# Moving the first layer's token sums of squares behind the fifth weight piece on the scalar engine

## The reference

```python
def rms_norm(x, g):
    xf = x.astype(jnp.float32)
    y = xf * lax.rsqrt(jnp.mean(xf * xf, axis=-1, keepdims=True) + RMS_EPS)
    return (y * g.astype(jnp.float32)).astype(x.dtype)

h = rms_norm(x, norm_g)
proj = jnp.einsum('bsd,de->bse', h, w_in)
(q_lat, kv_lat, z_a, dn_qkv, dn_a, dn_b, z_b, dil_qkv, z_c, gate_logits) = split_last(proj, IN_SPLITS)
...
mixed = jnp.sum(gates * branch_out, axis=2)
return x + jnp.einsum('bsd,de->bse', mixed, w_out)
```

## Time and profile before

| | |
|---|---|
| time, median of 3 runs (us) | 794.68 |
| time of the profiled execution (us) | 795.01 |
| its span, first to last instruction (us) | 793.0 |
| TensorE busy | 783.8 us, 99% |
| VectorE busy | 556.5 us, 70% |
| ScalarE busy | 478.9 us, 60% |
| GpSimd busy | 194.2 us, 24% |
| granted TensorE clock, mean | 1.000 |

### The profile page before, as it was taken

The page is one execution under the profiler, slowest core; times in us unless marked ns, Lnnn a source line. Parts: engine busy times, 40 slices in busy tenths (PEclk is TensorE's granted clock), DMA queues, the critical chain, the costliest instruction groups (busy, mean ns, idle before and its releaser), DMA issues.

```text
span 793.0 us, 15698 instructions
## 1 busy us (share of the span) xinstructions
PE 783.8 (99%) x6314; PEld 674.7 (85%) x6314; DVE 556.5 (70%) x748; ACT 478.9 (60%) x1077; POOL 194.2 (24%) x196
## 2 busy tenths in 40 slices
PE   7999999999999999999999999999999999999998
PEld 5999888878888888888899998888888888888886
DVE  6687878968376577676656887887865754957763
ACT  5769486676486554354457777765856756543551
POOL 1165104206032002421023511321331500116100
PEclk9999999999999999999999999999999999999999
DMA  8566454454563446465565563554455443654551
GB/s 236 194 191 210 158 145 136 146 160 129 140 185 114 140 126 197 122 196 173 157 196 179 157 197 111 166 171 147 125 156 149 122 146 107 185 185 141 181 184 54
DMA packets 73054, 125.15 MB, mean 158 GB/s; under 512 B 9757, under 2 KB 17047, under 8 KB 72983
## 3 DMA queue, kind: packets, MB, share of 16 engines
q1 hardware_dynamic: 72560, 124.10, 51.2%
q10 hardware_dynamic: 423, 0.06, 0.1%
HBM read 122.03 MB, written 1.05 MB: 155 GB/s over the span
## 4 chain that ended last, share of the span: by engine, by line
PE 93%; ACT 3%; DMA 1%; DVE 1%; issue 1%; SPq 0%; ACTq 0%
PE bank L781 23%; PE bank L783 22%; PE bank L782 22%; PE bank L763 3%; PE bank L765 3%; PE bank L764 3%; PE bank L872 2%; PE bank L925 1%; PE bank L811 1%; DMA raw<-in_w_in 1%; ACT w_hi L1162 1%; PE bank L886 1%; PE bank L920 1%; PE bank L902 1%; PE bank L1013 1%
## 5 line engine op out<-in xcount | busy, mean ns | idle before, releaser
L1500 DVE TENSOR_TENSOR w_lo<-raw,w_hi 128x1024 fp32r<-128x1024 f32 (+4 forms) x240 | 296.4, 1265 | 102.4 <-ACT w_hi L1162 100.1
L1162 ACT ACTIVATE w_hi<-raw 128x1024 fp32r<-128x1024 f32 (+4 forms) x239 | 234.7, 1018 | 83.7 <-PE bank L783 70.2
L781 PE MATMUL bank<-w_hi,hT 128*128 128x512 f32 (+2 forms) x704 | 278.0, 395 | 1.5 <-DVE w_lo L1500 0.7
L783 PE MATMUL bank<-w_hi,hT 128*128 128x512 f32 (+2 forms) x704 | 270.9, 385 | 0.0
L782 PE MATMUL bank<-w_lo,hT 128*128 128x512 f32 (+2 forms) x704 | 270.6, 384 | 0.0
L781 PEld LDWEIGHTS bank<-w_hi,hT 128*128 128x128 f32 x704 | 132.9, 189 | 26.8 <-issue 1.1
L783 PEld LDWEIGHTS bank<-w_hi,hT 128*128 128x128 f32 x704 | 132.7, 188 | 25.7
L782 PEld LDWEIGHTS bank<-w_lo,hT 128*128 128x128 f32 x704 | 133.0, 189 | 22.9
L1948 POOL TENSOR_TENSOR sm<-sm,tab 128x8 f32<-128x8 f32 (+3 forms) x46 | 58.9, 1280 | 183.4 <-ACT dn L1375 78.9
L763 PE MATMUL bank<-hT,w_hi 128*128 128x256 f32 x192 | 54.9, 286 | 0.0
L765 PE MATMUL bank<-hT,w_lo 128*128 128x256 f32 x192 | 54.3, 283 | 0.0
(11 more groups left out here) (236 smaller groups left out, 1000.3 us busy)
## 6 DMA issues: line engine op xcount, KB each, us to landing
raw<-in_w_in SPq DMA_DIRECT2D x168, 512.0 KB, 4.5
raw<-in_w_branch SPq DMA_DIRECT2D x24, 512.0 KB, 4.3
raw<-in_w_out SPq DMA_DIRECT2D x16, 512.0 KB, 4.2
raw<-in_w_in SPq DMA_DIRECT2D x8, 384.0 KB, 5.3
raw<-in_w_in SPq DMA_DIRECT2D x8, 320.0 KB, 4.6
raw<-in_mla_w_kv_b SPq DMA_DIRECT2D x8, 256.0 KB, 3.1
raw<-in_mla_w_q_b SPq DMA_DIRECT2D x4, 384.0 KB, 3.4
xs<-in_x SPq DMA_DIRECT2D x2, 512.0 KB, 5.6
```

The lines of the kernel that those rows point to most:

```text
L781: mm(o, src[0][:, a, tok], hi[:, k, :], start=starts and p == k == 0, stop=False)
L783: last = mm(o, src[1][:, a, tok], hi[:, k, :], start=False, stop=ends(u, p) and k == k1 - k0 - 1)
L1162: av(view(w_hi, q % SPLIT, k1 - k0, n), view(raw, q % RAW, k1 - k0, n), ACT.Copy).then_inc(hi_done, 1)
L1500: tt(view(w_lo, q % SPLIT, k1 - k0, n), view(raw, q % RAW, k1 - k0, n), view(w_hi, q % SPLIT, k1 - k0, n).bitcast(F32), ALU.subtract).then ...
```

## The change

The step `norm` of the first layer is taken out of the beginning of the list and put behind the `prep` of piece 4. The second layer's `norm` stays where it is.

```diff
     order = [(0, ("prep", 0, 0)), (0, ("xT", 0)), (0, ("prep", 0, 1)), (0, ("xT", 1)), (0, ("prep", 1, 0)), (0, ("prep", 1, 1)),
-             (0, ("xT", 2)), (0, ("xT", 3)), (0, ("norm",))]
+             (0, ("xT", 2)), (0, ("xT", 3))]
...
             order.append((layer, ("unit", u, 1)))
             order += ahead(layer, u, 0)
+            if u == layer == 0:
+                order.append((layer, ("norm",)))
             if whole(u) or UNITS[u][2] == 1:
```

## The result

The changed kernel takes 796.34 us, median of 20 runs (795.59 to 797.82); the kernel before, timed beside it, 794.60 us, median of 20 runs (794.07 to 795.88). The ratio is 1.0022 with a 95% interval of 1.0016 to 1.0028: 1.75 us slower, 1.3 to 2.2 by the interval. The prediction said 796.0, between 794.4 and 797.4, +1.3, and gave 0.63 to "no change that can be told" and 0.35 to "slower". The time lies in the range; the loss was put 0.45 us too small, and with it the ratio fell on the far side of the 0.2% line, to which the prediction had given 0.35 (the interval holds the line itself). Three of the 20 executions lie at 797.7 to 797.8, the rest at 795.6 to 796.7. The profiled execution is one of the three: 797.77 us, with a span of 795.7.

A forecast was written before the change was run, and what follows sets the result against it. TensorE was taken as the bound. The sixth piece's first matmul 1.22 us later plus 0.07 of pitch gave +1.3 us, so 796.3 for the profiled execution and 796.0 on the median of 794.68; range 794.4 to 797.4.

The forecast's parts named there:

- What bounds the kernel: TensorE, busy 99% of the span: time is its work plus idle gaps, and ScalarE edits count only through a gap.
- When the high part can begin: ScalarE's fifth-piece high part waits for its transfer, issued 9.98, taking 6.4 us, landing 16.38; ScalarE stands still until 16.40.
- The landing at 13.2: Fifth piece's landing by a 3.2 us transfer estimate for 384 KB; the prediction went by the profile's 6.4 us instead.
- What comes later, and what TensorE sees: Sixth piece's high part at 19.94, 1.61 later; TensorE waits 2.1 us for it, first matmul at 22.00, 1.22 later.
- What hides the rest: Later copies, roots, eviction and eighth to tenth pieces cost TensorE nothing; thinnest cover 1.0 us, at the tenth piece.
- Rival 2: Second stall: a tenth-piece transfer of 8.94 us makes it 1.8 late; +3.1 us, 797.8 us; chance 0.15.
- Rival 4: Partly given back: TensorE's two other waits for ScalarE, 0.5 us in all, could shrink; +0.8, 795.5 us; chance 0.09.
- Before, the sixth piece's first matmul ran at 20.78: TensorE's start on the sixth piece in the profile before; subtracted from 22.00 to give 1.22 later.
- Rival 1: Fifth piece lands by 14.8, so ScalarE never waits; -0.3 us, 794.4 us; chance 0.10.
- Rival 3: TensorE's 2.1 us gap drops its clock to 1.2 GHz for the rest of unit 2; +4.5, 799.2 us; chance 0.04.

The follow-up runs named there:

- gains_after: Changed kernel with the first layer's seven gain transfers issued behind pieces 6 and 7, not the fourth piece; 796.31 us, against 796.19 us for that shift without the change.
- no_wait: Changed order, but the fifth piece's high part is rounded from x instead of the weights, so ScalarE has nothing to wait for; 794.74 us, 1.0000 of the kernel before.
- again: The changed kernel run once more, unaltered; 796.30 us, ratio 1.0020 to the kernel before.
- split: Kernel before, with the second square moved behind the fifth and sixth pieces' high parts, copies, sine and first square left in place; 794.69 us, ratio 0.9999.
- wide: Changed kernel with one more square, its result unused, in front of the two squares, to widen TensorE's gap; 798.56 us, 1.0047 of the kernel before.
- wide_fill: As wide, plus five idle matmuls in front of TensorE's wait for the sixth piece; 796.96 us, 1.0029 of the kernel before.

## Why the prediction was right, and where it was not

- **What bounds the kernel.** Right. The ruler holds to 0.15 us over ten traces: all that changes ahead of t6 is carried to the end.
- **When the high part can begin.** Right to 0.01 us in the profile after: 16.40 as worked out from issue and transfer time. The landing is 16.1 to 16.6 in all twelve traces with the gain transfers in their old place. It is steadier than the two terms it was added from: the issue lies at 9.31 to 9.98 and the transfer takes 6.3 to 7.2 us, by and large the longer, the earlier it was issued. Nothing in the prediction said so; that the sum held is in part luck. The landing at 13.2 that I had worked out from the Trainium skill (DMA: Bandwidth & Descriptors, Bandwidth, and Latency and other measured facts) agrees with none of these traces; with the gain transfers moved away, the transfer took 3.5 us against the 3.2 of that estimate.
- **What comes later, and what TensorE sees.** Right: 19.94 worked out, 19.95 measured; 22.00 worked out, 21.88 and 21.96 measured (from the sixth high part to t6 it takes 1.93 us, not 2.06). The new wait is 2.1 us in the one trace, as predicted, and 1.1 in the other, where TensorE came later.
- **What hides the rest.** Right: roots to 21.91 (21.9 worked out), the eighth piece at 22.75 (22.8), and no wait at the eighth, ninth or tenth piece. Rival 2 did not come true in the changed kernel; only gains_after has such a wait, 0.6 us. Rival 4 did not either: the two waits of 0.2 us stayed.
- **The step that was mis-sized** is "Before, the sixth piece's first matmul ran at 20.78". That number is right for the profiled execution, but it was taken for the usual one, which by the ruler has 20.3. The prediction corrected for the execution's 0.33 us above the median by subtracting it from the level, 796.3 to 796.0, and kept the difference of 1.3. That is the mistake: what made before late in that execution (the fourth piece at 12.72, and the whole of ScalarE's queue behind it) is just what the changed kernel is blind to, because it waits for the fifth piece anyway. The correction belonged to the difference: 1.3 + 0.33 = 1.6, and the level stays 796.3. The measured values are 1.75 and 796.34.
- **Rival 1**, the early landing, was a sound mechanism: no_wait takes the wait away and with it the loss, and in the trace of gains_after the piece lands early and the gap is gone. In no trace with the gain transfers in their old place does the fifth piece land before 16.06, though in four of them it was issued over 0.6 us earlier than in the profile. With its -0.3 it was also too hopeful, since in the second trace of before there was no gap at the first matmul of unit 2 to win.
- **Rival 3**, the clock, was given 0.04 and +4.5 us in place of +1.3. It came in 3 of 31 executions at +1.5 on top of the rest (the prediction had 3.2, all 18 matmuls slow; ten were), and was what the first profile after showed. The argument against it, that the clock was at 2.4 GHz in the stretch with the widest gaps, was one trace's word: other traces have 0.74 to 0.77 there (again, split, wide). The Trainium skill (TensorE: Matmul & The Clock Gate, Part 1) has idleness lowering the clock; wide and wide_fill agree, 4 of 5 executions against none of 7.

## What to carry to other kernels

Before an instruction is moved forward in an in-order queue, work out when its input is there: if that is later than its new place, the engine stands still, and all that now stands behind it is delayed by that wait, less what it would have waited for its own input anyway (here 3.2 us of waiting cost about 1.8, because the sixth piece itself is there only near 18.1). The more work is moved behind it, the earlier the engine arrives and the longer it waits: half of the change cost 1.2, the whole 1.75. Where a predicted gain or loss hangs on a few tenths of a microsecond, take two or three traces of the kernel before, and ask of each cause of scatter whether the changed kernel feels it too. And a gap on TensorE of about 2 us can cost another 1.5 us in clock, in some executions only, so that one profile shows either case.

## What the runs showed that I had not expected

- The granted clock of the view can miss a slow stretch. In the trace of no_wait the 128x320 matmuls between 12 and 15 us have a pitch of 0.27 instead of 0.15 us, while the clock of that stretch reads 1.00:

```profile
12.28 0.47 PE L784 MATMUL bank<-w_lo,hT 128*128 128x320 f32 x1
12.55 0.47 PE L785 MATMUL bank<-w_hi,hT 128*128 128x320 f32 x1
```

```profile
12.00:16.00 4.00, 4.00 (x18) 3.56 (x18) 2.40 (x5) 3.53 (x12) 0.00 (x0) 1.00 0.98 255
```

- Seven small transfers of gains, under 0.4 MB together in the issue view, nearly doubled the time of a 384 KB weight transfer issued behind them: 6.3 to 7.2 us in twelve traces, 3.5 and 3.6 in the two where they had been moved away. Issued later they did the same to the ninth piece (512 KB, 6.0 and 7.7 us instead of 3.6), and there it cost more: the kernel became slower.
